# Differential attention: a head's eight score blocks in one visit of TensorE, and the next queries' raw values and squares ahead of the masks and exponents

## The reference, cut to what matters

```python
def diff_mixer(xn, k, v, w_q, q_gain, lam_params, head_gain, w_out, lambda_init):
    q = rms_norm((xn @ w_q).reshape(B, S, DIFF_HEADS, 2, DIFF_DH), q_gain) * (DIFF_DH ** -0.5)
    lam = jnp.exp(jnp.sum(lp[0] * lp[1])) - jnp.exp(jnp.sum(lp[2] * lp[3])) + lambda_init
    def attend(args):
        s = jnp.einsum('bhcqd,bhckd->bhcqk', q_blk, k)
        s = jnp.where(kpos[None, :] <= qpos[:, None], s, -jnp.inf)
        p = jax.nn.softmax(s, axis=-1)
        a = p[:, :, 0] - lam * p[:, :, 1]
        return jnp.einsum('bhqk,bhkv->bhqv', a, v)
    o = rms_norm(o, head_gain) * (1.0 - lambda_init)
    return o.reshape(B, S, DIFF_HEADS * DIFF_VD) @ w_out
```

## Time and profile before

| What | us |
|---|---|
| Median of 3 runs | 2217.99 (2217.99 to 2218.63) |
| Profiled execution: span | 2215.6 |
| Profiled execution: time of its own beside the span | not listed in the profile |
| PE, DVE, ACT busy | 2203.4, 1624.1, 1141.1 |
| First scores to the last step's last head sum | 1691.6 to 1842.5 |

### The profile page before, as it was taken

How to read it: one execution, slowest core, us unless ns; L and a number is a source line. 1 busy time by engine, 2 the same in 40 slices (tenths; PEclk the granted TensorE clock), 3 DMA queues, 4 the chain that set the end, 5 groups by cost and what they waited for, 6 DMA issues and landing times.

```text
span 2215.6 us, 32419 instructions
## 1 busy us (share of the span) xinstructions
PE 2203.4 (99%) x13130; PEld 1910.7 (86%) x13130; DVE 1624.1 (73%) x2428; ACT 1141.1 (52%) x1843; POOL 0.2 (0%) x4
## 2 busy tenths in 40 slices
PE   9999999999999999999999999999999999999999
PEld 7777899999778999998899888998987767898997
DVE  5755978787676969697777796776764777786774
ACT  5755644444475634355534563543555886543542
POOL 0000000000000000000000000000000000000000
PEclk9999999999999999999999999999999999999999
DMA  4222223232322223232311222222232112232222
GB/s 153 79 86 77 95 96 110 90 115 70 108 94 83 96 96 104 97 115 67 130 66 59 79 106 101 96 99 106 78 126 76 58 58 76 96 112 98 96 92 99
DMA packets 37300, 206.94 MB, mean 93 GB/s; under 512 B 4256, under 2 KB 4768, under 8 KB 17824
## 3 DMA queue, kind: packets, MB, share of 16 engines
q1 hardware_dynamic: 34560, 199.17, 25.6%
q10 hardware_dynamic: 2592, 5.70, 0.8%
HBM read 202.76 MB, written 2.10 MB: 92 GB/s over the span
## 4 chain that ended last, share of the span: by engine, by line
PE 93%; DVE 4%; ACT 2%; issue 1%; DMA 0%; ACTq 0%; DVEq 0%
PE ps L985 30%; PE ps L346 18%; PE ps L348 18%; PE ps L347 18%; PE ps L1508 2%; PE ps L2708 1%; PE ps L1563 1%; PE ps L1532 1%; DVE low_w L422 1%; PE ps L2239 1%; PE ps L1558 1%; ACT high_w L401 1%; PE ps L2727 1%; PE ps L1524 1%; PE ps L1214 1%
## 5 line engine op out<-in xcount | busy, mean ns | idle before, releaser
L422 DVE TENSOR_TENSOR low_w<-raw_w,high_w 128x2048 fp32r<-128x2048 f32 (+4 forms) x211 | 420.2, 1993 | 101.5 <-ACT high_w L401 101.3
L401 ACT ACTIVATE high_w<-raw_w 128x2048 fp32r<-128x2048 f32 (+4 forms) x211 | 352.1, 1670 | 147.7 <-DMA raw_w<-in_w_m_dn 93.8
L346 PE MATMUL ps<-ffn_hidh,high_w 128*128 128x512 f32 x864 | 336.6, 390 | 0.1
L347 PE MATMUL ps<-ffn_hidl,high_w 128*128 128x512 f32 x864 | 336.3, 389 | 0.0
L348 PE MATMUL ps<-ffn_hidh,low_w 128*128 128x512 f32 x864 | 336.1, 389 | 0.0
L985 PE MATMUL ps<-forms_th,forms_s 128*128 128x256 f32 x816 | 231.0, 283 | 1.9 <-ACT forms_kept L1031 1.9
L985 PE MATMUL ps<-xh,high_w 128*128 128x256 f32 x816 | 230.9, 283 | 0.0
L985 PE MATMUL ps<-xl,high_w 128*128 128x256 f32 x816 | 230.9, 283 | 0.0
L985 PE MATMUL ps<-xh,low_w 128*128 128x256 f32 x816 | 230.9, 283 | 0.0
L985 PE MATMUL ps<-forms_th,form_lows_s 128*128 128x256 f32 x816 | 230.9, 283 | 0.0
L985 PE MATMUL ps<-form_lows_t,forms_s 128*128 128x256 f32 x816 | 230.9, 283 | 0.0
(11 more groups left out here) (348 smaller groups left out, 4552.2 us busy)
## 6 DMA issues: line engine op xcount, KB each, us to landing
raw_w<-in_w_f_gu SPq DMA_DIRECT2D x44, 1024.0 KB, 4.8
raw_w<-in_w_m_up SPq DMA_DIRECT2D x32, 1024.0 KB, 4.8
raw_w<-in_w_m_dn SPq DMA_DIRECT2D x24, 1024.0 KB, 4.8
raw_w<-in_w_f_dn SPq DMA_DIRECT2D x8, 1024.0 KB, 4.8
raw_w<-in_w_m_dn SPq DMA_DIRECT2D x16, 512.0 KB, 3.4
raw_w<-in_w_b_qk SPq DMA_DIRECT2D x8, 1024.0 KB, 4.8
raw_w<-in_w_f_dn SPq DMA_DIRECT2D x8, 896.0 KB, 4.6
raw_w<-in_w_f_dn SPq DMA_DIRECT2D x16, 448.0 KB, 3.2
```

What stands on the lines that cost most here:

```text
L346: pe.matmul(out, sh, mh, start=start, stop=False)
L347: pe.matmul(out, sh, ml, start=False, stop=False)
L401: act.activation(wh[slot][:, 0:elems], raw[slot][:, 0:elems], ACT.Copy).then_inc(w_rounded, 1)
L422: dve.tensor_tensor(wl[slot][:, 0:elems], raw[slot][:, 0:elems], wh[slot][:, 0:elems].bitcast(F32), ALU.subtract).then_inc(w_split, 1)
```

## The change

On PE: `step` makes all queries of the next head first, with the key sums after 3 k-tiles where `key_split(p)` holds (1 before) and after 2 elsewhere, then `head_sum`, then the last two k-tiles, then all eight score blocks in one visit. The blocks get places of their own: blocks 0 and 2 in bank 5, 1 and 3 in bank 6, block 4 in bank 1 (that of the keys), 5 to 7 in banks 2 to 4. The keys of the next head therefore wait for the mask of block 4, and the transposes for that of block 3 instead of block 4. In the last step, the second group of output projections (`out_first((1, 0), ...)`) comes after the scores and the first transposes.

On ACT: `place_values` and `square(nx, 0)` come ahead of the exponents, and `head_root` after the first `copy_pt`. On DVE: `raw(nx, 0)` comes ahead of the masks, `square_low(nx, 0)` ahead of the last two masks, `split_weights` ahead of `head_scale`, and `raw(nx, 1)` ahead of the first two combines in every step. The first two masks wait for the block that shares their bank.

```diff
-    F_BANK = (2, 3, 4, 5, 6, 2, 3, 4)
+    KEY_BANK = 1
+    F_PLACE = ((5, 0), (6, 0), (5, P), (6, P), (KEY_BANK, 0), (2, 0), (3, 0), (4, 0))
+
+    def diff_block(n):
+        bank, at = F_PLACE[n]
+        return ps[:, bank, at:at + (n // 2 + 1) * P]
...
+            if first == 0 and p and which == KEY_BANK:
+                pe.wait_ge(F["masked"], 8 * (p - 1) + 5)
...
-        def scores(p, st, rows_of):
-
-            if rows_of[0] == 0:
-                pe.wait_ge(F["q_staged"], p + 1)
-                pe.wait_ge(F["k_staged"], p + 1)
-                if p == 0:
-                    pe.wait_ge(F["v_staged"], 8)
-            for i in rows_of:
+        def scores(p, st):
+
+            pe.wait_ge(F["q_staged"], p + 1)
+            pe.wait_ge(F["k_staged"], p + 1)
+            if p == 0:
+                pe.wait_ge(F["v_staged"], 8)
+            wait_past(pe, F["masked"], 8 * p)
+            wait_past(pe, F["pt_copied"], TB * (p - 1))
+            for i in range(TB):
                 for hh in range(2):
-                    n = 2 * i + hh
-                    wait_past(pe, F["masked"], 8 * p + n - 4 if n > 4 else 8 * (p - 1) + min(n + 6, 8))
                     rows = slice(64 * hh, 64 * hh + 64)
-                    pe.matmul(ps[:, F_BANK[n], 0:(i + 1) * P], FQ[st][rows, i * P:(i + 1) * P],
+                    pe.matmul(diff_block(2 * i + hh), FQ[st][rows, i * P:(i + 1) * P],
                               FK[st][rows, 0:(i + 1) * P], start=True, stop=True).then_inc(F["scored"], 1)
 
         def turn_p(p, st, blocks):
...
-                pe.wait_ge(F["masked"], clip(8 * (p + 1) + 5, 8 * NHD))
+                pe.wait_ge(F["masked"], clip(8 * (p + 1) + 4, 8 * NHD))
...
                 if k == 0:
                     pe.wait_ge(F["logged"], 2 * NHD - 1 + j)
+                    if j == KEY_BANK:
+                        pe.wait_ge(F["masked"], 8 * (NHD - 1) + 5)
...
         def step(p, st, nx, prev):          # PE
             if nx:
-                head = 1 if key_split(p) else 2
+                head = 3 if key_split(p) else 2
                 made(nx[0], 0, 0, head)
                 sums(p, 1)
                 made(nx[0], 0, head, 6)
             else:
                 sums(p, 1)
                 out_first((0, 0), (0, 1), (0, 2))
-            scores(p, st, (0, 1))
+            if past_two(p):
+                head_sum(p - 2)
             if nx:
                 made(nx[0], 0, 6, KD)
-            else:
-                out_first((1, 0), (1, 1), (1, 2))
-            if past_two(p):
-                head_sum(p - 2)
-            scores(p, st, (2, 3))
+            scores(p, st)
             if prev:
                 turn_p(*prev, (0, 1))
+            if not nx:
+                out_first((1, 0), (1, 1), (1, 2))
             if nx:
                 made(nx[0], 1, 0, 4)
                 sums(nx[0], 0)
...
         def step(p, st, nx, prev):          # ACT
             if nx:
                 round_weights(act, st_diff.base + p + 2)
-            else:
+            if prev:
                 place_values(prev[0])
-            exps(p, st, (0, 1))
             if nx:
                 square(nx[0], 0)
-            else:
+            exps(p, st, (0, 1))
+            if not nx:
                 rounded(4)
-            if past_two(p):
-                head_root(p - 2)
             exps(p, st, (2,))
             if prev:
                 copy_pt(prev[0], (0, 1))
+            if past_two(p):
+                head_root(p - 2)
             exps(p, st, (3,))
             if prev:
                 copy_pt(prev[0], (2, 3))
-            if prev and nx:
-                place_values(prev[0])
...
-                dve.wait_ge(F["scored"], 8 * p + n + 1)
+                dve.wait_ge(F["scored"], 8 * p + n + (3 if i == 0 else 1))
...
         def step(p, st, nx, prev):          # DVE
             if past_two(p):
                 head_low(p - 2)
-            mask(p, st, (0, 1))
             if nx:
                 raw(nx[0], 0)
+            mask(p, st, (0, 1, 2))
+            if nx:
+                square_low(nx[0], 0)
             else:
                 split(3, 4)
-            mask(p, st, (2, 3))
+            mask(p, st, (3,))
             if nx:
-                square_low(nx[0], 0)
+                split_weights(dve, st_diff.base + p + 2)
             if past_two(p):
                 head_scale(p - 2)
+            norm(p, st)
             if nx:
-                split_weights(dve, st_diff.base + p + 2)
-            norm(p, st)
-            if p == 0:
                 raw(nx[0], 1)
             combine(p, st, (0, 1))
-            if prev and nx:
-                raw(nx[0], 1)
```

More of the change, by code:

```diff
@@ L2991, in mask @@
                 stand_alone(dve.tensor_tensor_reduce(
-                    f_probs(2 if hh else st, i), ps[:, F_BANK[n], 0:(i + 1) * P],
+                    f_probs(2 if hh else st, i), diff_block(n),
                     f_causal[:, TOK - (i + 1) * P:TOK], -0.125, 3e38, ALU.add, ALU.min,
```

## The result

| | median, us | runs |
|---|---|---|
| before | 2218.53 (2217.99 to 2218.84) | 6 |
| changed | 2224.61 (2224.16 to 2227.07) | 6 |

The ratio is 1.003, 95% interval 1.002 to 1.004: slower by 6.1 us. The profiled execution took 2224.16 us with a span of 2222.0, so 2.2 lie around the span, and the span grew by 6.4. Two of the six runs of the changed kernel took 2226.79 and 2227.07 us at a mean granted clock of 0.999, the other four 2224.16 to 2224.80 at 1.000.

What follows compares the result with a forecast made beforehand. PE, busy 99% of the span, was taken to bound the kernel. Terms 5.2 + 0.2 - 0.2 + 1.3 = +6.5 on 2217.99 gave 2224.5 us, +0.29%; 2221.0 to 2227.8 was to hold 8 in 10.

Steps and rivals of the forecast that it cites:

- The head sum's wait: PE before the head sum, p = 2 to 6: chain 3.81 us, cover 2.29, so 1.52 wait plus 0.08 restart.
- Wait (a): PE at the key sums: 0.32 a head lost waiting for squared keys' low part, gone in p = 2 to 6.
- Visit start to keys: PE from the score visit's start to the next keys: 3.0 us, 0.15 of it lost to the fifth mask.
- The visit itself: All eight score blocks on PE: 2.55 us, from 0.85 plus 1.70; one entry and exit saved, 0.20 a head.
- The sum for p = 2 to 6: Five middle steps: +1.60 - 0.32 - 0.20 - 0.19 + 0.15 = +1.04 us each, +5.2 together.
- p = 0 and 1: First two steps: +0.2 us for p = 0, including 0.45 of fifth-mask wait, and -0.2 for p = 1.
- The last step: p = 7: head sum 1.1 us late, later scores and exponents, P-V waiting about 1 us; +1.3 in all.
- ACT's margin: Before P-V: ACT's copies of the transposes end at 9.6, PE comes at 10.1; hidden by 0.5 us, costed at nothing.
- Rival B: ACT's exponents end 0.8 us later, P-V waits 0.3 in five heads, tail 1 more: 2227 us; chance 12%.
- rival D: After PE waits of 1.5 us in each step, matmuls run at 1.2 GHz: +10, 2234 us; chance 3%.
- The banks: By the skill's bank rotation, separate places save at most 0.19 a head; sum 5 x 0.15 lower, 2223.7 us.
- A: In p = 2 to 7 the head sum does not wait, only savings are left: -3.1, 2214.9 us; chance 7%.

Runs made afterwards that it cites:

- Experiments 1 to 3: Changed kernel, separately: head sum behind the last query k-tiles, 2218.06 us; key sums behind two k-tiles, 2221.68; output square and head's low part ahead of key work, 2218.47.
- experiment 4: Kernel before, with key sums behind two k-tiles instead of one where they stood behind one: 2216.52 us, ratio 0.9993.
- experiment 8: Experiment 5 plus, in the last step, the head sum behind the scores: 2215.63 us, ratio 0.9989; second sample 2216.11 us, 0.9991.
- experiment 9: Experiment 8 plus, in step p = 6, the raw keys of head 7 behind the first two combines again: 2215.74 us, ratio 0.9989.
- experiment 6: Experiment 5 with scores in two visits again, blocks 0 to 3 ahead of the last query k-tile, 4 to 7 behind the head sum: 2218.29 us.
- experiment 7: Experiment 5 with ACT's and DVE's order around the masks put back as in the kernel before: 2223.64 us, ratio 1.0022.
- Experiment 5: Changed kernel with key sums behind two query k-tiles and head sum behind all eight: 2216.95 us, ratio 0.9994.

## Why the prediction was right

Predicted 2224.5, measured 2224.61. That the totals meet within 0.1 us is partly luck: the forecast growth was 6.5 on a median of 2217.99, the measured one 6.1 on 2218.53 (6.4 by the spans). By its steps, from the two traces:

- *The head sum's wait.* Predicted 1.52 and 0.08 for the restart in each of p = 2 to 6. Measured 1.50 (1.73 less the pitch of 0.23) and 0.09 (its second matmul follows 0.32 after the first instead of 0.23). Experiments 1 to 3 show both ends of the chain and its length: 3.80, 3.81, and 2.56 when two of its links were taken out.
- *The terms beside it.* Wait (a) is gone, 0.32: experiment 4 shows it alone. Visit start to keys was predicted as 3.0 and is 3.01, but parted otherwise. The visit itself needs 2.35 us, not 2.55: so it measures in the last step of experiment 8, where the head sum follows without waiting (2.36 in experiment 9). The transposes start at 2.54, so they wait about 0.19 for the fourth mask, which I had at nothing, and the keys 0.18 more for the fifth, where I had 0.15. One saving and one wait that I left out, 0.2 each, cancel: that is luck.
- *The sum for p = 2 to 6* was +5.2; it is +5.46 (1720.40 to 1821.32 against 1720.78 to 1816.24). Four steps are 1.02 to 1.04 longer. Step p = 5 has a third of a microsecond on top: its visit takes 2.88 to the transposes instead of 2.54, in this and in every other version with one visit, and DVE has 0.55 between the starts of its first two masks there where 0.21 is usual. Why stays open; with two visits (experiment 6) it is not there.
- *p = 0 and 1.* Predicted 0 together, measured -0.24: p = 0 +0.09, p = 1 -0.33. The first mask starts 1.06 and 1.09 after the visit there, not 1.15, and the keys come 2.89 and 2.92 after it, not 3.0.
- *The last step.* Predicted +1.3, measured +1.36 (27.34 against 25.98 from key sums to the tail's last head sum). The size was right and the inside not. Of the 1.1 at the head sum only 0.5 is lost right before it (0.72 after the matmul before it, less the pitch), because PE has lost 0.66 already ahead of the first output projection, which starts 1.29 after the key sums instead of 0.63. Its split stands behind the combines that the moved raw keys push back: with the raw keys behind them again it is 0.76 (experiment 9). The two together are 1.15, since the end of the chain sets when the head sum can start, however much PE idles before. Nor does P-V wait about 1 us there, but 0.24: most of the 1.36 is lost by then.
- *ACT's margin.* Predicted 0.5 before P-V in steps 2 to 6; the copies of p = 4 end at 1777.82 and P-V starts at 1778.63: 0.8. Rival B had no ground in these steps.
- *The clock.* In the profiled execution it is 1.00 in a step with 1.35 us of idle PE, and 1.00 over 1688 to 1850: rival D did not come there. The Trainium skill ("TensorE: Matmul & The Clock Gate", A second HAM failure mode) warns of a clock that oscillates with frequent short idles; this trace shows none with waits like these. The two runs at 0.999 have no trace, so whether the clock fell in them after such a wait is open; experiment 7 shows that it does after one of 2.18 us.
- *The banks.* By the advice of the Trainium skill to rotate matmul groups through PSUM banks ("Perfetto Trace Analysis", Optimizing Tensor Performance) the sum would have been 2223.7, an estimate. The keys' wait of 0.18 to 0.19 that it leaves out is in the trace, and experiment 7 shows how it grows to 0.78 when DVE comes later to that one bank.

The rival that mattered, A, was the same change with the wait taken away: 2214.9 by my sum. Experiment 5 comes part of the way, with the last step's loss still in it, at 2216.95; experiment 8, which takes most of that loss away too, measures 2215.63 and 2216.11.

## What to carry to other kernels

When PE is 99% busy, a saving of 0.2 us in each of eight turns shows in the trace, but so does every instruction moved ahead of work that covered its operand. Before a consumer is moved, write down the chain that ends in it, from the instruction that really starts it, and count the PE work left between the two. Here the chain was 3.8 us long and hung on the key sums by a shared tile, so that moving the key sums later and the head sum earlier took from the same cover twice; moving the consumer behind six matmuls gave all of that back, its producer ahead of three half of it. And try the small edit alone first: the key sums moved by one k-tile in the kernel before (experiment 4) gave as much as the whole re-ordering with both cures (experiment 5).

## What the runs showed of the hardware

- A value made by a 128x512 operation on DVE lets the waiting matmul go 0.82 to 0.84 us after that operation starts, in every kernel here (1765.93 to 1766.77 in the changed one); from the second key-sum matmul to ACT's first operation on the sums it is 0.42 to 0.44 (1762.97 to 1763.40). That constancy is why a hand sum over links came within a few hundredths.
- Sixteen score matmuls in one visit took 2.35 us to the next matmul that had nothing to wait for (experiment 8), where two visits of eight took 0.85 and 1.70.
- Idle of 1.35 us in each 20 us did not lower the granted clock in the profiled execution of the changed kernel. After a single wait of 2.18 us in experiment 7 it was 0.50, and matmuls of 512 columns started 0.43 apart; later in that step it was 1.00 again.
